# Expert weights in 2 MB loads of 16 KB pieces, an eight-pass gather, splits on VectorE, and an earlier signal from the gate

## What is computed

```
def moe(x, w_router, b_router, w_gate_up, b_gate_up, w_down, b_down):
    logits = jnp.dot(x, w_router).astype(f32) + b_router.astype(f32)
    top_val, top_idx = lax.top_k(logits, TOP_K)          # 4 of 32 experts for each row
    gates = jax.nn.softmax(top_val, axis=-1)
    ...
    def expert_block(args):
        xb, e = args
        gu = jnp.dot(xb, w_gate_up[e]) + b_gate_up[e]     # 1024 x 2048 weights
        g = jnp.minimum(gu[:, :D_FF], SWIGLU_LIMIT)
        up = jnp.clip(gu[:, D_FF:], -SWIGLU_LIMIT, SWIGLU_LIMIT)
        hdn = (up + 1.0) * (g * jax.nn.sigmoid(SWIGLU_ALPHA * g))
        return jnp.dot(hdn, w_down[e]) + b_down[e]        # 1024 x 1024 weights
    ...
    y = jnp.einsum('tkd,tk->td', out_rows[dest].reshape(T, TOP_K, -1).astype(f32), gates)
```

## Time and profile before

| | us |
|---|---|
| median of 3 runs | 1305.03 (1304.78 to 1305.94) |
| the profiled execution | 1302.26 |
| its span, to which all rows refer | 1300.5 |
| PE busy in the span | 1244.7 (96%) |
| DVE, ACT, POOL busy | 466.5, 169.7, 254.3 |
| bytes moved | 440.89 MB |

### The profile page before, as it was taken

The page is one execution under the profiler, slowest core; times in us unless marked ns, Lnnn a source line. Parts: engine busy times, 40 slices in busy tenths (PEclk is TensorE's granted clock), DMA queues, the critical chain, the costliest instruction groups (busy, mean ns, idle before and its releaser), DMA issues.

```text
span 1300.5 us, 22589 instructions
## 1 busy us (share of the span) xinstructions
PE 1244.7 (96%) x7932; PEld 565.4 (43%) x7933; DVE 466.5 (36%) x923; ACT 169.7 (13%) x299; POOL 254.3 (20%) x444
## 2 busy tenths in 40 slices
PE   7999998999599999999999999999999999999996
PEld 4666666667433333343333333433333333333332
DVE  6757757231732222232222222322222223222224
ACT  4741015112300000000000000000000000000002
POOL 1157750000421111112111111121111111211100
PEclk9989999999699999999999999999999999999999
DMA  8323332497379999999999999999999999999995
GB/s 224 98 66 98 98 97 72 138 321 291 146 306 422 421 421 422 422 422 422 422 422 422 423 422 422 423 422 422 423 422 422 422 422 422 422 422 422 422 422 216
DMA packets 97120, 440.89 MB, mean 339 GB/s; under 512 B 16100, under 2 KB 45312, under 8 KB 47936
## 3 DMA queue, kind: packets, MB, share of 16 engines
q1 hardware_dynamic: 94720, 439.31, 83.8%
q10 hardware_dynamic: 2368, 1.15, 0.3%
HBM read 437.97 MB, written 1.87 MB: 338 GB/s over the span
## 4 chain that ended last, share of the span: by engine, by line
PE 79%; DVE 9%; DMA 5%; ACT 3%; SPq 2%; issue 2%; POOL 0%; DVEq 0%; POOLq 0%; ACTq 0%
PE psum L830 32%; PE psum L868 16%; PE psum L493 13%; PE psum L810 7%; DMA big<-in_w_gate_up_dram 4%; PE psum L749 3%; PE psum L471 2%; SPq L369 2%; DVE m L1659 2%; DVE m L1662 2%; DVE m L1656 2%; ACT m L1128 1%; PE psum L505 1%; PE psum L840 1%; PE psum L592 1%
## 5 line engine op out<-in xcount | busy, mean ns | idle before, releaser
L830 PE MATMUL psum<-big,m 128*64 128x512 f32 x2048 | 473.1, 597 | 1.9 <-DVE m L1639 1.2
L1646 DVE TENSOR_TENSOR acc<-acc,psum 128x512 f32<-128x512 f32 (+1 forms) x192 | 123.1, 682 | 572.5 <-PE psum L810 572.5
L830 PEld LDWEIGHTS psum<-big,m 128*64 128x64 f32 x2048 | 137.6, 136 | 303.0 <-issue 282.7
L868 PE MATMUL psum<-big,m 128*64 128x512 f32 x1024 | 226.8, 595 | 0.0
L493 PE MATMUL psum<-big,m 128*128 128x320 f32 x576 | 165.4, 442 | 2.7 <-DVE big L1288 1.0
L1245 POOL COPY m<-uT 96x64 bf16 x32 | 7.5, 234 | 675.1 <-PE psum L854 674.8
L493 PEld LDWEIGHTS psum<-big,m 128*128 128x128 f32 x576 | 108.5, 193 | 53.9 <-issue 12.7
L868 PEld LDWEIGHTS psum<-big,m 128*64 128x64 f32 x1024 | 71.3, 137 | 134.2 <-issue 129.5
L810 PE MATMUL psum<-m 64*128 64x512 f32 (+1 forms) x384 | 106.7, 632 | 0.0
L1128 ACT ACTIVATE m<-m 128x512 f32<-128x512 f32 x32 | 20.2, 632 | 580.4 <-DVE m L1656 580.4
L796 PE MATMUL psum<-m 128*128 128x64 bf16 x2376 | 76.8, 195 | 5.6 <-POOLq L1241 5.6
(11 more groups left out here) (258 smaller groups left out, 826.3 us busy)
## 6 DMA issues: line engine op xcount, KB each, us to landing
big<-in_w_gate_up_dram SPq DMA_DIRECT2D x256, 1024.0 KB, 21.7
big<-in_w_down_dram SPq DMA_DIRECT2D x128, 1024.0 KB, 23.4
m<-in_w_in_dram SPq DMA_DIRECT2D x18, 1024.0 KB, 5.3
m<-in_w_s_glu_dram SPq DMA_DIRECT2D x8, 512.0 KB, 4.4
m<-in_w_out_dram SPq DMA_DIRECT2D x4, 1024.0 KB, 10.9
acc<-in_x_prompt_dram SPq DMA_DIRECT2D x4, 512.0 KB, 5.1
m<-in_w_ml_out_dram SPq DMA_DIRECT2D x2, 1024.0 KB, 5.0
out_dram<-acc SPq DMA_DIRECT2D x2, 512.0 KB, 2.7
```

The source lines that it names most:

```text
L830: mm = pe.matmul(psum[SLOT * hf:SLOT * hf + SLOT, GB + gu, :], xeT[:, c, :], big[:, base:base + 512], start=(c == 0), stop=(c == GU_CHUNKS ...
L868: mm = pe.matmul(psum[SLOT * hf:SLOT * hf + SLOT, DB, :], hT[:, m, half, :], big[:, base:base + 512], start=False, stop=(c == DN_CHUNKS - ...
L1646: v.tensor_tensor(x, x, psum[0:n, CB + hf, :], ALU.add).then_inc(S("added"), 1)
```

## The change

Four things are changed at once.

1. The ring has 8 slots of 2 MB (`WIDE`), the same space as before. An expert is 6 loads: 4 of `w_gate_up` with two neighbouring rows for a partition, and 2 of `w_down` with four. A piece is 16 KB long. The channel order of everything that meets these weights follows: `xm` is written in two halves of even and odd channels, `w_router` is read the same way, `hm` is read with a step of 4. `chunks_used` counts 2 MB.
2. The middle part of the third tile lies in the unused lower half of its top part, and `tab` holds that tile's ranks twice, so that one pass serves both: 8 passes (`PARTS`), 64 matmuls. ScalarE makes one copy more for it, and the router's and the ranks' matmuls of this tile are done twice, once for each half of the partitions.
3. Both subtractions of the split are on VectorE, and the first is done in place in `xm`. The ring's last slots, which share that space, are loaded only after the last part is written (`parts_ready`, `mid_ready`), not after `rest`.
4. In the last chunk of gate and up the gate's two halves raise `gate_done`, and VectorE's clamp of the gate waits for that; the clamp of up still waits for `chunks_used`.

```diff
-RING = 16
-GU_CHUNKS, DN_CHUNKS = DK, FK // 2
+WIDE = 2 * CHUNK
+RING = 8
+GU_CHUNKS, DN_CHUNKS = DK // 2, FK // 4
...
-                src = a["w_gate_up"][0, bass.ds(e, 1), c * P:(c + 1) * P, :].rearrange("a p n -> p (a n)")
+                row = 2 * c * P
+                src = a["w_gate_up"][0, bass.ds(e, 1), row:row + 2 * P, :].rearrange("a (p k) n -> p (a k n)", k=2)
...
-                    for c in ((0, 1, 2), (3, 4, 6), (7, 8, 9), (10, 11))[g - 24]:
+                    for c in ((0,), (1, 3), (4,), (5,))[g - 24]:
...
-            sp.wait_ge(S("rest"), 3)
+            sp.wait_ge(S("parts_ready"), 3)
+            sp.wait_ge(S("mid_ready"), 4)
...
-                    for i in range(3):
-                        for q in range(3):
-                            mm = pe.matmul(psum[:, XB, k * SLOT:(k + 1) * SLOT], parts[:, q, i, k * P:(k + 1) * P], pb[:, i, :],
+                    for n, (q, i) in enumerate(PARTS):
+                        mm = pe.matmul(psum[:, XB, k * SLOT:(k + 1) * SLOT], parts[:, q, i, k * P:(k + 1) * P], pb[:, i, :],
...
+                                if c == GU_CHUNKS - 1 and k == 1 and gu == 0:
+                                    mm.then_inc(S("gate_done"), 1)
...
-                nc.gpsimd.tensor_tensor(rest[0:n, i, :], xm[i][0:n, :], parts[0:n, 0, i, :], ALU.subtract).then_inc(S("rest"), 1)
...
+                v.tensor_tensor(xm[i][0:n, :], xm[i][0:n, :], parts[0:n, 0, i, :], ALU.subtract).then_inc(S("rest"), 1)
...
+                    dve.wait_ge(S("gate_done"), g + 1)
+                    v.tensor_scalar(gm, psum[:, GB, :], LIMIT, None, ALU.min).then_inc(S("gu_read"), 1)
                     dve.wait_ge(S("chunks_used"), CHUNKS * g + (CHUNKS + GU_CHUNKS))
-                    v.tensor_scalar(gm, psum[:, GB, :], LIMIT, None, ALU.min).then_inc(S("gu_read"), 1)
```

More of the change, by code:

```diff
@@ L245, in hybrid_stream_step @@
         nmb = w.take(D)
+        PARTS = [(q, i) for i in range(2) for q in range(3)] + [(0, 2), (2, 2)]
         rest = cut(m2[:, CHUNK:CHUNK + 3 * D], 3, D)
@@ L766, in logits @@
                 for k in range(DK):
-                    mm = pe.matmul(psum[0:n, i, 0:NE], xnT[:, k, t0:t0 + n], wrt[:, k, :],
-                                   start=(k == 0), stop=(k == DK - 1))
+                    for at in range(0, P, n):
+                        mm = pe.matmul(psum[at:at + n, i, 0:NE], xnT[:, k, t0:t0 + n], wrt[:, 2 * (k % 4) + k // 4, :],
+                                       start=(k == 0), stop=(k == DK - 1), skip_group_check=True)
                 mm.then_inc(S("logits"), 1)
@@ L783, in _ @@
                     before = cst[0:nb, C_TRI:C_TRI + n] if b == i else ones[0:nb, 0:n]
-                    pe.matmul(psum[0:n, 4, i * NE:(i + 1) * NE], before, msk[0:nb, b, :], start=(b == 0), stop=(b == i))
+                    for at in range(0, P, n):
+                        pe.matmul(psum[at:at + n, 4, i * NE:(i + 1) * NE], before, msk[0:nb, b, :],
+                                  start=(b == 0), stop=(b == i), skip_group_check=True)
             for b in range(3):
@@ L826, in expert @@
                         pe.wait_ge(S(f"w_landed{slot(r, c)}"), 16 * loads(turn_, r, c))
[L827 to L831, removed]
@@ L1197, in _ @@
             pool.wait_ge(S("mix_ready"), 8)
[L1198 to L1201, removed]
+            do(nc.gpsimd.memset(parts[64:128, 2, 2, :], 0.0))
             pool.sem_inc(S("zeros_set"), 1)
@@ L1206, in _ @@
                 pool.sem_inc(S(name), n)
[L1208 to L1219 removed]
+            pool.wait_ge(S("ss"), 6)
             pool.wait_ge(S("group_used"), 28)
@@ L1560, in _ @@
                     turned_rows(0)
+                    first_rest(0)
                 inv = inverse_rms(i, n, 1)
@@ L1572, in of @@
             def of(i):
-                n = TILES[i][1]
-                return [n] + [x[0:n] for x in top[i]]
+                return [P] + list(top[i])
             for group in ((0,), (1, 2)):
+                if group == (1, 2):
+                    first_rest(2)
                 for i in group:
@@ L1608, in _ @@
                     v.tensor_scalar(f8[:, 8:9], t8[:, 0:1], -1.0, None, ALU.mult).then_inc(S("top_ready"), 1)
+            last_rest(0)
             dve.wait_ge(S("ranks"), 1)
-            dve.wait_ge(S("zeros_set"), 2)
-            for i, (t0, n) in enumerate(TILES):
-                do.start(v.scalar_tensor_tensor(out=tab[0:n, :, i], in0=psum[0:n, 4, i * NE:(i + 1) * NE], scalar=1.0, in1=msk[0:n, i, :],
+            for i in range(3):
+                do.start(v.scalar_tensor_tensor(out=tab[:, :, i], in0=psum[:, 4, i * NE:(i + 1) * NE], scalar=1.0, in1=msk[:, i, :],
                                                 op0=ALU.add, op1=ALU.mult))
@@ L1623, in _ @@
             dve.sem_inc(S("cum_ready"), 1)
+            last_rest(1)
+            last_rest(2)
             for i, (t0, n) in enumerate(TILES):
-                lg, t8, i8, f8 = (x[0:n] for x in top[i])
+                n, lg, t8, i8, f8 = of(i)
                 dve.wait_ge(S("top_exp"), i + 1)
```

79 lines of the change are left out of this document (49 added, 30 removed).

## The result

| | before | after |
|---|---|---|
| median of the runs | 1305.49 us (4 runs) | 1293.95 us (4 runs) |
| the profiled execution, its span | 1302.26, 1300.5 | 1295.13, 1293.3 |

The ratio of the runs is 0.9913, with a 95% interval from 0.9902 to 0.9925: 11.5 us less, where 8.7 were forecast (1293.95 us against 1296.3). Between the two profiled executions the span fell by 7.2 us only. The profiled execution of before happened to be 3 us faster than the median of its fellows and that of after 1 us slower, so a single pair of traces does not carry the difference to the last microseconds. On two other chips the changed kernel came out at 0.9928 (0.9915 to 0.9941) and 0.9918 (0.9906 to 0.9931); by the medians that is 9.75 and 10.1 us less.

A forecast was written before the change was run, and what follows sets the result against it. The weight stream was taken to set the end, with TensorE almost level; −11.8 (rate) + 1.8 (start) + 1.5 (tail) − 0.2 (first block) = −8.7 us, from 1305.03 to 1296.3 us, within 1286.5 to 1308.5.

The forecast's parts named there:

- What bounds the kernel: Whole kernel: weight stream sets the end, TensorE almost the same; 29.8 against 28.83 us a block; the smaller gain counts.
- The sum: Whole kernel: −11.8 + 1.8 + 1.5 − 0.2 = −8.7 us, from 1305.03 to 1296.3 us.
- The rate: Weight stream: 16 KB pieces lift 422 GB/s to 427.5, worth −11.8 us.
- rival A: Weight stream: rate stays 422, a limit of HBM or port; only coarser steps remain, +3.1, 1308.1 us; chance 0.14.
- The 2 MB steps: Start and tail of the stream: restart after the whole first 2 MB, +1.8 us; larger steps at the end, +1.5 us.
- The gap: Between up and down: earlier gate signal and shorter gather cut 2.99 to 2.5 us, 0.49 us a block, mostly hidden by the stream.
- The first block: Routing and start: list of blocks 2.3 us earlier, 2.2 us given back before the gather; about −0.2 us, within ±2.
- Two things that the profile was to show: Steady part: SP's slot waits end near 800 to 900 us; TensorE's weight waits begin near 1050, some 9 us in all.

The follow-up runs named there:

- The two halves alone: Kernel before with only 2 MB loads of 16 KB pieces, 1304.13 us; changed kernel with 1 MB loads of 8 KB pieces, 1304.29 us; before 1304.88 us.
- rest_only: Changed kernel with the weights back in 1 MB loads of 8 KB pieces (ring of 16): 1304.29 us, 0.9995 of the kernel before.
- wide_8k: Changed kernel, 2 MB loads kept, each partition's 16 KB as two 8 KB pieces from rows apart: 1308.97 us, 1.0031 of the kernel before.
- no_gate: Changed kernel with the clamp of the gate waiting for chunks_used again: 1303.17 us, 0.9989 of the kernel before.
- wide_4k: Changed kernel, 2 MB loads kept, each partition's 16 KB as four 4 KB pieces: 1332.93 us, 1.0218 of the kernel before.

## Why the prediction was right

**What bounds the kernel: right, and now shown.** The text said that the stream sets the end, that TensorE sets almost the same end, and that the smaller gain counts. The two halves alone gave 0.75 and 0.6 us, together 9.75.

**The sum: close, and in part by luck.** By the medians of one chip, going from the kernel before over `rest_only` and `wide_8k` to the changed kernel, the terms are −0.6 for parts 2 to 4, +4.7 for the 2 MB steps and −13.8 for the rate, −9.75 in all; the prediction had −0.2, +3.3 and −11.8, −8.7. Each of the two large terms was short by 1.4 to 2 us, and the two errors stand on opposite sides.

**The rate: a little under-sized.** I forecast 427.5 GB/s, and it is 428 to 429. The estimate came from a straight line through 1 KB and 8 KB pieces, which had 6.9 ns for each piece. The three sustained rates, 410, 422 and 428.4, have 9.3 ns. By that line a piece of 1 KB would take 47.0 ns and run at 349 GB/s, where the burst of four microseconds had 365: either its rate is rough or the line ends somewhere below 4 KB, which no run settles. It gave the slope a little too high and the cost of a piece too low. The term was −11.8; measured between `wide_8k` and the changed kernel it is −13.8. The doubt whether 422 was a limit of HBM (rival A), fed by a short burst at 428, was unfounded: 16 KB pieces hold 428 to 430 from 420 us to the end of the stream. What the Trainium skill's figure of 512 B for line rate ("DMA: Bandwidth & Descriptors", Specifications) would have made of it, no gain at all, does not hold here: from 4 KB to 16 KB the rate still rose from 410 to 428.

**The 2 MB steps: under-sized by nearly a third.** +1.8 and +1.5 were forecast, 4.7 were measured. At the end the sum was right: the last gate and up load landed at 1264.5, down ended 14.7 us later, where 14.5 stood. The start was not: there the first 2 MB went at a lower clock (5.35 us), which the prediction did not have, and the stream filled up more slowly behind them. From 363 to 420 us it moved 382 GB/s where it was 396 (clock, DMA share and GB/s stand last; `before` first):

```profile
363.00:420.00 57.00, 56.54 (x386) 21.27 (x384) 15.70 (x26) 3.23 (x6) 10.34 (x24) 1.00 0.98 396
```

```profile
363.00:420.00 57.00, 57.00 (x372) 22.17 (x370) 15.90 (x26) 3.23 (x6) 10.45 (x25) 0.99 0.94 382
```

**The gap: right in its mechanism, 0.57 us instead of 0.49.** The order of events was as told: the gather ends last, the transposes wait for nothing. The gather is 0.23 us shorter and the wait of 0.23 is gone, as forecast. What I missed is that a wait costs TensorE more than its length, since the work behind it no longer overlaps with the work before: another 0.18 (0.74 against 0.56 us from one end to the next). Against it stand the 0.09 that down's start lost to 2 MB chunks, which was not foreseen and whose cause is open. That a wait costs more than its length is also why `no_gate` lost 8 to 10 us and not 0.5 to 2; the expectation had the right chain and the wrong size. The strided read of `hm` cost nothing that shows: the four transposes took 0.72 us in the timeline, and 0.74 before.

**The first block: nearly right; its first 2 MB were not.** The block began at 360.20, 0.7 us earlier than before, where 0.2 ± 2 was forecast. The list of blocks came 2.5 us earlier (2.3 forecast), and VectorE gave back the rest before the copy of the rows. This rests on one pair of traces; the changed kernel's other two began at 360.77 and 360.74. But the idle time on TensorE that this leaves had a price in clock, 1.7 us, and the first 2 MB were used at 365.55, 1.0 us later than the 364.56 of before.

**Two things that the profile was to show were wrong.** SP's waits for slots did not end near 800 to 900 us; they last to the end. And TensorE's waits for weights began near 915 and not 1050, and were 49.1 us in all and not some 9. What TensorE lost by them is less, the 12.7 us of the block lengths above. The text had read SP's silence after 950 us in the kernel before as every free slot being already ordered. It was not so. Late in the stream of the kernel before SP spent 19.0 us on issuing eight 1 MB loads:

```profile
1199.72 19.03 SPq L369 DMA_DIRECT2D big<-in_w_gate_up_dram  x8
```

That is 2.4 us each, where the stream needs 2.485, so its own instructions went at the pace of the stream. A load landed 26 us after its issue, which is 11 MB at 422 GB/s, of a ring of 16. With half the pieces for each MB SP waits for TensorE in 85 of 100 us (50.2 for gate and up as shown above, 34.6 for down). This did not touch the sum.

**Parts 2 and 3.** The pass left out is worth 0.24 us a block, which the stream hides for the most part, and for the splits no gain is shown. The change lives from the pieces and from one semaphore.

## What to carry to other kernels

When a transfer stream and an engine are both full, measure the length of a block undisturbed and the time that the stream needs for one. The gain of any change is then the smaller of two differences, and two changes that each measure as nothing may be ten microseconds together; test them in pairs before either is thrown away. Make pieces longer (16 KB were the longest tried) by giving a partition neighbouring rows and letting the order of channels follow. Signal from the matmul that finishes a half, not from the end of the chunk.

## What the runs showed of the hardware

- A piece of 4 to 16 KB has a fixed cost of some 9.3 ns in time of its DMA engine beside 37.7 ns for each KB: 410, 422 and 428 GB/s with 4, 8 and 16 KB. Loads of 1 MB and of 2 MB, both in 8 KB pieces, run at the same 422.
- With 4 KB and 8 KB pieces the issuing queue itself went at the pace of the stream, with 16 KB pieces it did not. In `wide_4k` SP stands in the chain in the middle of the stream, with 4.7 and 5.1 us for the issue of one load of 2 MB, which takes 5.1 us at 410 GB/s:

```profile
724.70 4.71 SPq L372
...
729.66 5.08 SPq L372
```

- TensorE pays more for a wait than the wait: in a row of work four transposes end 0.56 us behind the matmul ahead of them, after 0.46 us of idleness they need 0.75. After 2.6 to 3.0 us of idleness before the first block it worked some 3 to 5 us of its first 2 MB at the lower clock (5.35 to 5.93 us instead of 3.65, eight traces), after 1.2 to 1.4 us of idleness at the full clock (five traces).
- VectorE operations of 4 and 32 elements for a partition take 1.5 to 2.1 us beside GpSimd's subtractions of 1024 elements, and 0.2 to 0.3 us without them.
